# Gate and up products of the same 128 columns done as one pair, k by k, in a two-block fp32 transformer kernel

## The reference, cut to what matters

```python
def conv_glu_ffn(h, w_up_act, w_up_lin, w_conv, b_conv, w_down):      # first block, once a layer
    a = causal_depthwise_conv(h @ w_up_act, w_conv, b_conv)            # 3 taps over time
    return (jax.nn.gelu(a) * (h @ w_up_lin)) @ w_down

def _swiglu(h, wg, wu, wd):                                            # second block, twice a layer
    return (jax.nn.silu(h @ wg) * (h @ wu)) @ wd
```

## Time and profile before

| | us |
|---|---|
| median of 3 runs (2566.01 to 2570.57) | 2570.34 |
| profiled execution: time | 2570.5 |
| profiled execution: span of the core | 2568.7 |
| TensorE busy | 2438.7 (95%) |
| VectorE busy | 1742.6 (68%) |
| ScalarE busy | 1079.9 (42%) |
| GpSimd busy | 362.9 (14%) |
| mean DMA rate | 164 GB/s |

### The profile page before, as it was taken

How to read it: one execution, slowest core, us unless ns; L and a number is a source line. 1 busy time by engine, 2 the same in 40 slices (tenths; PEclk the granted TensorE clock), 3 DMA queues, 4 the chain that set the end, 5 groups by cost and what they waited for, 6 DMA issues and landing times.

```text
span 2568.7 us, 34574 instructions
## 1 busy us (share of the span) xinstructions
PE 2438.7 (95%) x13194; PEld 2045.1 (80%) x13194; DVE 1742.6 (68%) x2562; ACT 1079.9 (42%) x1846; POOL 362.9 (14%) x413
## 2 busy tenths in 40 slices
PE   3889999899999999999989999999999999999998
PEld 3678987779988878878658887888888888777997
DVE  6976886967995886786975475676575676345554
ACT  3466554566554212226745322224322324344543
POOL 1101111011111100103841110110100100000101
PEclk9999999999999999999999999999999999999999
DMA  7655886545774563552102254443353453322662
GB/s 302 214 163 199 286 304 215 206 155 196 252 262 145 182 219 123 195 191 83 58 33 71 94 176 152 156 164 123 115 200 112 164 186 109 119 75 78 186 199 92
DMA packets 135012, 420.91 MB, mean 164 GB/s; under 512 B 28352, under 2 KB 32576, under 8 KB 134848
## 3 DMA queue, kind: packets, MB, share of 16 engines
q1 hardware_dynamic: 134288, 416.98, 47.7%
q10 hardware_dynamic: 560, 1.72, 0.2%
HBM read 417.54 MB, written 1.11 MB: 163 GB/s over the span
## 4 chain that ended last, share of the span: by engine, by line
PE 61%; DVE 5%; ACT 2%; issue 1%; POOL 1%; DVEq 0%; POOLq 0%; ACTq 0%
PE ps L1126 19%; PE ps L1128 19%; PE ps L1127 19%; PE ps L1330 2%; DVE sl L1677 1%; PE ps L1310 1%; DVE F L1795 1%; DVE mjunk L1691 1%; POOL ap L2188 1%; ACT F L1452 1%; PE ps L1290 1%; PE ps L1279 0%; DVE ps L2032 0%; PE ps L1353 0%; PE ps L1320 0%
## 5 line engine op out<-in xcount | busy, mean ns | idle before, releaser
L1126 PE MATMUL ps<-hH,sh 128*128 128x256 f32 (+1 forms) x2560 | 842.0, 329 | 7.2 <-DVE hL L1766 3.6
L1128 PE MATMUL ps<-hH,sl 128*128 128x256 f32 (+1 forms) x2560 | 836.8, 327 | 0.0
L1127 PE MATMUL ps<-hL,sh 128*128 128x256 f32 (+1 forms) x2560 | 836.7, 327 | 0.0
L1393 ACT ACTIVATE sh<-raw 128x1024 fp32r<-128x1024 f32 x534 | 540.9, 1039 | 418.1 <-PE ps L1128 320.0
L1677 DVE TENSOR_TENSOR sl<-raw,sh 128x1024 fp32r<-128x1024 f32 x534 | 644.7, 1232 | 83.1 <-ACT sh L1393 82.2
L1691 DVE CUSTOM_DVE_ANT_0 mjunk<-raw,cB,V 128x1024 bf16<-128x1024 f32 x384 | 543.2, 1414 | 31.9 <-DMA C<-in_cst 8.5
L1126 PEld LDWEIGHTS ps<-hH,sh 128*128 128x128 f32 x2560 | 480.8, 188 | 60.5 <-issue 9.1
L1127 PEld LDWEIGHTS ps<-hL,sh 128*128 128x128 f32 x2560 | 483.4, 189 | 49.2 <-issue 1.7
L1128 PEld LDWEIGHTS ps<-hH,sl 128*128 128x128 f32 x2560 | 481.6, 188 | 48.2
L2161 POOL TENSOR_TENSOR uLl<-F,uHh 128x256 fp32r<-128x256 f32 (+1 forms) x132 | 163.5, 1239 | 1188.8 <-ACT uHh L1566 1091.6
L1126 PE MATMUL ps<-sh,uHh 128*128 128x512 f32 x792 | 313.3, 396 | 9.7 <-DVE sl L1677 9.6
(11 more groups left out here) (164 smaller groups left out, 2114.4 us busy)
## 6 DMA issues: line engine op xcount, KB each, us to landing
raw<-in_w SPq DMA_DIRECT2D x756, 512.0 KB, 4.6
G<-gates SPq DMA_DIRECT2D x14, 512.0 KB, 6.5
raw<-in_w SPq DMA_DIRECT2D x16, 256.0 KB, 4.0
cB<-in_rpb SPq DMA_DIRECT2D x64, 64.0 KB, 2.7
X<-in_x ACTq DMA_DIRECT2D x1, 1024.0 KB, 11.9
X<-in_ctx SPq DMA_DIRECT2D x1, 1024.0 KB, 8.0
out<-X SPq DMA_DIRECT2D x2, 512.0 KB, 2.6
raw<-in_w SPq DMA_DIRECT2D x2, 288.0 KB, 6.0
```

The costliest lines, as they stand in the source:

```text
L1126: self.e.matmul(out, lh, rh, start=start, stop=False)
L1127: self.e.matmul(out, lh, rl, start=False, stop=False)
L1128: return self.e.matmul(out, ll, rh, start=False, stop=stop)
L1393: self.e.activation(self.m["sh"][k % SPL][:, 0:w], self.m["raw"][r % RAW][:, 0:w], ACT.Copy).then_inc(self.sems["w_hi"], 1)
```

## The change

A new step `twin` makes both products of a pair together: for each k three matmuls for the one bank and then three for the other, 48 matmuls in all. It waits for the low halves of both units and for both banks before its first matmul, and both banks become full within the last six matmuls. It stands for the two calls of `product` in `ffn1` (F1, F2; all 22 pairs) and in `ffn2` (G1 to G3: pairs 3 to 10 of the first half and 0 to 10 of the second; G4: all 22). In `ffn1` the late parts of the pair before, which stood one behind each product, now both stand behind the pair.

```diff
+    def twins(self, names, idx, c0, cols, act):
+        units = [self.unit(True, [(name, idx, k, c0, 128) for k in range(KD)]) for name in names]
+        banks = [self.bank() for _ in names]
+        self.add("twin", unit=units[1], units=units, banks=banks, cols=cols, act=act, last=True)
+        return banks
...
         for c in range(KF):
-            ba = self.product("w_up_act", l, c * 128, slice(0, 256), ("h", hid))
-            if late:
-                late.pop(0)()
-            bu = self.product("w_up_lin", l, c * 128, slice(0, 256), ("h", hid))
-            if late:
-                late.pop(0)()
+            ba, bu = self.twins(("w_up_act", "w_up_lin"), l, c * 128, slice(0, 256), ("h", hid))
+            for x in late:
+                x()
...
-                    ba = self.product("ffn_w_gate_2", (l, half_i), cc * 128, slice(0, N), ("h", hid))
-                    bu = self.product("ffn_w_up_2", (l, half_i), cc * 128, slice(0, N), ("h", hid))
+                    ba, bu = self.twins(("ffn_w_gate_2", "ffn_w_up_2"), (l, half_i), cc * 128, slice(0, N), ("h", hid))
...
                 if s.get("last", True):
-                    used.add(s["unit"])
+                    used.update(s.get("units", [s["unit"]]))
...
+    def twin(self, s):
+        cols = s["cols"]
+        w = cols.stop - cols.start
+        H, L = self.m["hH"], self.m["hL"]
+        parts = []
+        for n, b in zip(s["units"], s["banks"]):
+            self.wait_ge(self.gone(b))
+            parts.append((n, b, self.buf(b)[:, 0:w], *self.weights(n)))
+        for k in range(KD):
+            self.act_ready(s["act"], k, range(cols.start // 128, cols.stop // 128))
+            c = slice(k * 128, (k + 1) * 128)
+            for n, b, out, hi, lo in parts:
+                x = self.mm3(out, hi[:, c], lo[:, c], H[:, k, cols], L[:, k, cols], k == 0, k == KD - 1)
+                if k == KD - 1:
+                    x.then_inc(self.sems["mm"], 1)
+                    self.done("mm", ("full", b), ("w_used", n), ("act_used", s["act"]))
```

More of the change, by code:

```diff
@@ L1114, in __init__ @@
         Engine.__init__(self, *a)
-        self.parts = dict(start=self.start, proj=self.proj, prod=self.prod, down=self.down, turn=self.turn,
+        self.parts = dict(start=self.start, proj=self.proj, prod=self.prod, twin=self.twin, down=self.down, turn=self.turn,
                           qturn=self.qturn, idx=self.idx, att_q=self.att_q, att_t=self.att_t, att_o=self.att_o,
```

## The result

The changed kernel takes 3022.23 us (median of 4 runs, 3019.04 to 3030.3), the kernel before 2568.18 in the same comparison: a ratio of 1.1777, 95% interval 1.1756 to 1.1798. The forecast was 3025. The profiled execution has a span of 3028.5 us.

The account below looks back on a forecast made before the run. TensorE, busy in every microsecond of the pairs, was taken to bound the kernel, so late low halves add one for one. 2570.5 of the profiled execution + 362 of waits + 92 of clock = 3025 us, range 2925 to 3085.

Parts of the forecast that it names:

- a wait of G1, two jobs and both low halves: G1: TensorE idles from pair end through Silu, multiply, two jobs and both low halves on DVE, 9.87 us.
- a wait of G2 or G3, one job: G2, G3: TensorE idles through Silu, multiply, one job and one low half, 5.6 us (5.1 to 5.97).
- G1: Added waits in G1: 15 pairs awaiting both low halves, plus each half's first down unit, 165.5 us together.
- F1: Added waits in F1: late units behind two two-job pairs, a down unit and the loop, 21.5 us.
- F2: Added waits in F2: low halves late where 13 pairs have a job of two instructions, 13.9 us.
- clock: TensorE's granted clock falls behind idle times of 2.5 us and more: 46 waits at 2.0, 92 us.
- hL, alternation: TensorE in the pairs: switching two banks and touching k 4 to 7 later cost 0; hL at most 8.1 us.
- The look-ahead: DVE's order: counting units by number, it reaches only the next pair with two jobs, so low halves come late.
- the loop: F1, F2: low halves, multiply, split, L1548 and taps take 7.06 us with a two-instruction job, against 5.655 a pair.
- The full clock behind waits: Rival: the waits come but TensorE's clock stays up behind them, 2933 us; chance 0.12.
- Longer waits: Rival: POOL's split stretches two job instructions a pair, and each wait costs the longest low clock, 3090 us; chance 0.11.
- No wait: Rival: in G1 the low halves behind the multiply serve the pair after next, 2562 to 2570.5 us; chance 0.04.

Follow-up runs that it names:

- e1: The changed kernel with the look-ahead of a two-unit step longer by two numbers (8 for 6): 2604.49 us, 1.0131 to the kernel before.
- e2: The changed kernel with pending low halves put right behind the two-unit step, ahead of the multiply and jobs: 2585.82 us, 1.0054 to the kernel before.
- e4: The changed kernel with the look-ahead of a two-unit step longer by one number (7): 2756.94 us, 1.072 to the kernel before.
- e3: The changed kernel, but TensorE does one bank after the other, awaiting the second unit only before its own matmuls: 2830.69 us, 1.1007 to the kernel before.
- e6: The kernel before, with both late parts in F1 and F2 emitted behind the second product: 2586.54 us, 1.0061 to the kernel before.
- e5: The changed kernel with 36 useless matmuls at the head of 15 waiting pairs of G1: 2987.46 us, 1.1621 to the kernel before.
- e9: The kernel before with gate and up together in G1 to G4 only, low halves right behind that step: 2570.2 us, 1.0 to the kernel before.
- e8: The kernel before with pending low halves right behind every product and down step, ahead of jobs and additions: 2579.01 us, 1.0035 to the kernel before.
- e10: The kernel before with pending low halves right behind the first three w_down units of each half, F and G: 2554.95 us, 0.9944 to the kernel before.
- e7: The kernel before with gate and up together in F1 and F2 only: 2622.76 us, 1.0202 to the kernel before.

## Why the prediction was right

Step by step, forecast and measured:

| step | forecast | measured |
|---|---|---|
| a wait of G1, two jobs and both low halves | 9.87 | 9.26 and 9.33 |
| a wait of G2 or G3, one job | 5.6 (5.1 to 5.97) | 5.47 to 5.65 |
| G1 | 165.5 | 155.9 |
| G2 | 77.8 | 75.0 |
| G3 | 83.4 | 80.8 |
| F1 | 21.5 | 21.2 |
| F2 | 13.9 | 16.8 |
| all waits, added | 362 | 349.7 |
| clock | 92 (46 waits at 2.0) | 109.9 (48 waits, 2.3 each) |
| hL, alternation | 0 | 0.1, 0 |

The measured waits of a stage are those that were added: what the kernel before waited there is taken off, 6.8 us in G1, 2.6 in G2 and 1.3 in F2. The 109.9 is all that TensorE's busy time grew by; the granted clock alone accounts for 107.4 of it.

**The look-ahead** was the cause, as said: e1 and e2 take the waits away by two different edits, e4 gives the half dose, and e3 shows that more than half of the loss needs neither the alternation nor one wait for both units.

**The single wait was 0.5 us too long**, 9.87 for 9.43 from the time when the pair should have begun (9.26 of that are idle). I let the Silu start at the pair's end, as a link of the chain: 0.04 + 0.63 us from there to the multiply. It needs the gate bank alone, and with the alternation that is full three matmuls before the pair's end. It runs from 893.58 to 894.18, while the up bank's last matmul starts at 893.85; the multiply starts at 894.34, 0.26 us behind 894.08, where the next pair should have begun. That is 0.4 us less. POOL's split stretched a job to 2.05 us and not 2.19, which is 0.1 more: from the multiply on, 6.67 us to the low halves stand against 6.80. From the low halves' end to TensorE are 0.15 us and not 0.04.

**F1 and F2.** In F1 the waits of two jobs and of one behind them were forecast at 5.33 and 4.01; TensorE's starts are 5.37 and 3.93 us further apart there than within a pair, twice. In F2 the loop was worth 13.9 by the recurrence and 12.2 by the trace (1.3 of that was there before), and e6 has it alone, also 12.2. What I had not in the sum is one wait of 5.9 us:

```profile
655.03 1.28 ACT L1419 ACT_TABLE_LOAD   x1
659.04 1.92 ACT L1419 ACTIVATE cB<-cB 128x2048 f32<-128x2048 f32 x1 [2.73 <-DMA cB<-in_cc]
...
661.09 1.28 DVE L1710 CUSTOM_DVE_ANT_0 mjunk<-raw,cB,V 128x1024 bf16<-128x1024 f32 x1 [5.04 <-ACT cB L1419]
```

It was in the profile of before, where DVE idled 4.19 us for the same ACT instruction, hidden by the pair of slack:

```profile
627.27 1.28 DVE L1691 CUSTOM_DVE_ANT_0 mjunk<-raw,cB,V 128x1024 bf16<-128x1024 f32 x1 [4.19 <-ACT cB L1400]
```

I took DVE's work behind a pair from pairs in which nothing else happened. Where cover goes, every idle time of DVE that it hid has to be priced, and that one was not.

**The clock** was the term that was mis-sized: 110 for 92. The number of waits was right (48 of 2.5 us and more in place of 46), the price was 2.3 and not 2.0. My seven rows held four short falls of 1.4 to 1.7 us; over all twelve stretches of lower clock in the trace of before the mean is 2.5 and the most 3.9, so 2.9 was not the upper end either. Behind the waits of 9.3 us the loss is between 1.5 and 3.0. e5 measures the price directly: 34.8 / 15 = 2.3 us. The Trainium skill's rule that the ramp is worth under 1% of a typical kernel's span (TensorE: Matmul & The Clock Gate, What's actually happening) does not fit this kernel: it was 110 of 2570 us, 4.3%, since the ramp comes back with every wait, as that page's section on oscillation describes. By that rule the time would have been 2958, and the trace disagrees by 64 us.

**The errors offset each other**: 12 us too much in the waits, 18 too little in the clock. That the time came out within 3 us of 3025 (and the profiled span, 3028.5, within 4) is luck to that extent.

**The rivals.** The full clock behind waits (2933) is refuted by the windows and e5. The one row that spoke for it, behind the wait of 18.5 us at the start, was misread. TensorE's rows there, in the kernel before:

```profile
40.58 0.63 PE L1127 MATMUL ps<-sl,hH 128*128 128x512 f32 x1
41.00 0.63 PE L1128 MATMUL ps<-sh,hL 128*128 128x512 f32 x1
...
44.72 0.40 PE L1128 MATMUL ps<-sh,hL 128*128 128x512 f32 x1
44.95 0.39 PE L1126 MATMUL ps<-sh,hH 128*128 128x512 f32 x1
```

Ten starts in a row, to 44.41, are 0.43 us apart, as at the lower level; the trace has no record of the granted clock before 44.6 us, and the view shows such a stretch as 1.00. So that row spoke neither for this rival nor for 0 as the lower end.

Longer waits (3090): the split stretched one instruction a pair in G1, not two. No wait (not slower) needs the low halves of the pair after next in the place behind the multiply; e9 is that case, by another edit and with F left alone, and gives 2570.2, inside the 2562 to 2570.5 which that rival said it would be worth.

**Two statements were wrong without an effect on the sum.** G4's pairs took 5.44 us before, not 5.655 (59.86 us for 528 matmuls in the earlier trace rows, 0.1134 each); I had carried over F's. And the pairs that the change touches have 5,904 matmuls, 912 of them in G1, not 5,300 and 800.

## What to carry to other kernels

A look-ahead that counts steps or numbers, and not time or instructions, changes when steps are merged: after such an edit look in the order at what stands on each helper engine between two instructions that wait for the bottleneck, and ask whom it serves. Anything that the bottleneck needs next must stand ahead of the instruction that waits for it; then price the rest of that queue, table loads and fetched vectors too. Placing it first everywhere is no rule either: e8 did, and lost 9 us. And a wait costs the clock behind it, here 2.3 us on top of 9.3; in e10 3.3 us of lower clock went with two waits of 2.5 us.

## What the runs showed of the hardware

- Alternating two banks every three matmuls costs nothing measurable: 1.0 (0.9986 to 1.0013) in e9.
- Idle times of 1.1 to 1.2 us, as in the 15 filled pairs of e5, leave the granted clock at its full level; those of 9.3 us bring the lower one behind the wait, with matmuls 0.43 us apart. Of those in between, one of 1.9 us in F1 of the changed kernel is followed by the lower level (1.7 us lost), and those of 1.4 us in F2 are not.
- The same matmuls of 256 columns, at a granted clock of 1.00, have starts 0.1178 us apart in some stretches and 0.1134 in others, and which it is differs between executions. F1 has the same order in the kernel before and in e10, whose first edited place lies behind it. Before (PE alone, 511 matmuls in 60 us), and below it e10 (532):

```profile
240.00:300.00 60.00, 60.00 (x511) 1.00 0.81 260
...
240.00:300.00 60.00, 60.00 (x532) 1.00 0.82 266
```

  In e10 it changes to the slower spacing in the middle of F1, at about 312 us. G4 in the changed kernel has the slower one, where the earlier trace rows has the faster:

```profile
2835.96:2896.00 60.04, 60.04 (x510) 60.04 (x511) 27.45 (x32) 27.64 (x42) 9.52 (x10) 1.00 0.54 173
```

  It isn't the alternation, since the kernel before has the slower spacing in F1 without it. For the 22 pairs of such a stage it is some 5 us, a part of what runs of one kernel differ by here (2562 to 2577 us in e9) and of the small differences in e7 and e10; what sets it stays open.
